# Up products by seven block products in the first and third MLP, behind two ordinary pairs of tiles

## The reference, cut to what matters

```python
# first block                         D_MODEL = SEQ = 1024, D_FF = 4096
hn = rms_norm(h, norm_mlp_w)
h = h + jnp.square(jax.nn.relu(hn @ w_up)) @ w_down
...
# third block
h = rms_norm_3(x, norm2_pre) * (1.0 + scale2) + shift2
f = jnp.square(jax.nn.relu(h @ w_fc1)) @ w_fc2
x = x + gate2 * rms_norm_3(f, norm2_post)
```

## Time and profile before

| | us |
|---|---|
| median of 3 runs | 3459.06 (3456.13 to 3461.45) |
| profiled execution | 3452.28 |
| its span | 3450.5 |
| TensorE busy | 3377.7 (98%) |
| VectorE / ScalarE / GpSimd busy | 1741.4 / 1064.7 / 1238.0 |
| mean granted TensorE clock | 0.991 of full speed |

### The profile page before, as it was taken

The page is one execution under the profiler, slowest core; times in us unless marked ns, Lnnn a source line. Parts: engine busy times, 40 slices in busy tenths (PEclk is TensorE's granted clock), DMA queues, the critical chain, the costliest instruction groups (busy, mean ns, idle before and its releaser), DMA issues.

```text
span 3450.5 us, 39435 instructions
## 1 busy us (share of the span) xinstructions
PE 3377.7 (98%) x16634; PEld 2748.7 (80%) x16634; DVE 1741.4 (50%) x2140; ACT 1064.7 (31%) x1565; POOL 1238.0 (36%) x662
## 2 busy tenths in 40 slices
PE   8999999999999999999999999999999999999998
PEld 6887877887888878765788888888878788888887
DVE  5553375555665468486545445445554631222224
ACT  5432243333112221475332212212332432222222
POOL 3212364555343123313323344344222343333333
PEclk9999999999999999999999999999999999999999
DMA  3112312226454111210212122232211211111113
GB/s 112 37 53 67 119 43 110 106 114 220 177 179 144 69 66 49 74 60 1 86 49 68 58 95 92 68 98 78 86 43 37 77 49 49 49 49 49 48 47 128
DMA packets 94044, 276.51 MB, mean 80 GB/s; under 512 B 13846, under 2 KB 20774, under 8 KB 93740
## 3 DMA queue, kind: packets, MB, share of 16 engines
q1 hardware_dynamic: 93868, 273.99, 23.3%
HBM read 239.18 MB, written 34.78 MB: 79 GB/s over the span
## 4 chain that ended last, share of the span: by engine, by line
PE 91%; DVE 5%; ACT 2%; POOL 1%; DMA 1%; issue 0%; SPq 0%; POOLq 0%; DVEq 0%; ACTq 0%
PE ps L669 25%; PE ps L670 25%; PE ps L672 25%; PE ps L727 3%; PE ps L729 3%; PE ps L728 3%; PE ps L869 1%; PE ps L1128 1%; PE ps L699 1%; PE ps L1177 1%; PE ps L701 1%; PE ps L700 1%; PE ps L1161 1%; DVE P L2711 1%; ACT T L1835 1%; PE ps L1114 0%
## 5 line engine op out<-in xcount | busy, mean ns | idle before, releaser
L3091 POOL TENSOR_TENSOR wlo<-raw,whi 128x1024 fp32r<-128x1024 f32 (+3 forms) x302 | 612.8, 2029 | 1510.2 <-ACT whi L1401 1510.1
L669 PE MATMUL ps<-HH,whi 128*128 128x512 f32 (+1 forms) x2464 | 973.4, 395 | 7.9 <-POOL HL L3097 3.1
L670 PE MATMUL ps<-HL,whi 128*128 128x512 f32 (+1 forms) x2464 | 963.1, 391 | 0.0
L672 PE MATMUL ps<-HH,wlo 128*128 128x512 f32 (+1 forms) x2480 | 767.2, 391 | 0.0
L1401 ACT ACTIVATE whi<-raw 128x1024 fp32r<-128x1024 f32 (+3 forms) x302 | 268.0, 888 | 1249.6 <-PE ps L672 1103.0
L669 PEld LDWEIGHTS ps<-HH,whi 128*128 128x128 f32 (+1 forms) x2464 | 461.7, 187 | 109.6 <-POOL HL L3097 3.5
L672 PEld LDWEIGHTS ps<-HH,wlo 128*128 128x128 f32 (+1 forms) x2480 | 464.3, 187 | 102.3 <-issue 0.6
L670 PEld LDWEIGHTS ps<-HL,whi 128*128 128x128 f32 (+1 forms) x2464 | 461.7, 187 | 98.2 <-issue 1.8
L669 PE MATMUL ps<-GH,whi 128*128 128x512 f32 x1256 | 493.1, 393 | 0.6 <-POOL wlo L3091 0.6
L670 PE MATMUL ps<-GL,whi 128*128 128x512 f32 x1256 | 488.8, 389 | 0.0
L2142 DVE TENSOR_TENSOR X<-ps,X 128x1024 f32<-128x1024 f32 (+1 forms) x155 | 186.2, 1203 | 490.8 <-PE ps L672 489.0
(11 more groups left out here) (440 smaller groups left out, 4166.9 us busy)
## 6 DMA issues: line engine op xcount, KB each, us to landing
raw<-in_w_up SPq DMA_DIRECT2D x76, 512.0 KB, 3.4
raw<-in_w_in SPq DMA_DIRECT2D x70, 512.0 KB, 3.3
raw<-in_w_fc SPq DMA_DIRECT2D x64, 512.0 KB, 3.3
raw<-in_w_down SPq DMA_DIRECT2D x32, 512.0 KB, 4.5
T<-in_w_ada SPq DMA_DIRECT2D x32, 512.0 KB, 4.3
raw<-in_w_fc SPq DMA_DIRECT2D x64, 256.0 KB, 2.7
hsc<-T SPq DMA_DIRECT2D x24, 512.0 KB, 2.6
raw<-in_w_down SPq DMA_DIRECT2D x40, 256.0 KB, 2.6
```

The costliest lines, as they stand in the source:

```text
L669: e.matmul(o_[0:m, half(hf)], whi_[:, k, :], hi[k0 + k][:, half(hf)], start=first, stop=False)
L670: e.matmul(o_[0:m, half(hf)], whi_[:, k, :], lo[k0 + k][:, half(hf)], start=False, stop=False)
L672: i = e.matmul(o_[0:m, half(hf)], wlo_[:, k, :], hi[k0 + k][:, half(hf)], start=False, stop=last)
L3091: e.tensor_tensor(wlo_of(name), raw_of(name), whi_of(name).bitcast(F), SUB).then_inc(*po.inc("lo " + name))
```

## The change

The four operands p4, p5, p6 and p7 get a place of their own in the G buffers, p1, p2 and p3 use the ordinary HH and HL. Both MLPs begin with four ordinary up tiles (two pairs), after which pairs 2 to 15 are block products. The combinations of operands are made between the norm and those pairs. Both then have 40 down tiles in five groups with 8, 8, 8, 4 and 4 input blocks, from hidden tiles that were written to DRAM and read back. The same functions now serve both MLPs, with a relu with bias on ACT in the third. The cut core of the diff:

```diff
+SIZES, FIRST = [8, 8, 8, 4, 4], [0, 8, 16, 24, 28]
+FAST = {f"{t}{f}" for t in DN for f in range(4, 32)}
+SPLIT = ("dn0_0", "fa2_0_0")
...
+    def phases(up, dn, t):
+        for f in range(32):
+            plan(f"{t}{f}", d[up][f])
+        for g in range(5):
+            for m in range(8):
+                plan(f"{DN[t]}{g}_{m}", d[dn][m, :, FIRST[g] * P:(FIRST[g] + SIZES[g]) * P])
...
+        OAT = {"p4": GO, "p7": GO + 16384, "p5": GO + 32768, "p6": GO + 49152}
+        OH = {p: at(f"OH{p}", OAT[p], [P, 4, 512], R) for p in OAT}
+        OL = {p: at(f"OL{p}", OAT[p] + 8192, [P, 4, 512], R) for p in OAT}
+        OF = {p: at(f"OF{p}", OAT[p] + 8192, [P, 4, 512]) for p in OAT}
...
+            for f in range(4):
+                job(f"up{f}", hhs, hls, lambda k: [dv(f"hl2 {k}")], 8, between=norm2 if f == 1 else None)
+                if f == 0:
                     sums("n2", dv("n2 acc7"))
-                elif (p, k) == ("p6", 2):
-                    spread_misc("n2 sp", one, dv("n2 r1"))
-            for n in range(16):
-                fast("up", n, ready=None if n else ready2, between=norm2 if n == 1 else None)
-            for n in range(32):
-                g, j = divmod(n, 8)
-                if (g, j) == (3, 0):
+            fast_all("up")
+            for n in range(40):
+                if n == 32:
                     lend("n3 sq")
-                job(f"dn{g}_{j}", ghs if g % 2 else hhs, gls if g % 2 else hls, lambda k: [either(f"dnl {8 * g + k}")], 8)
+                down("up", n)
                 row_step(n)
...
+            job("fa1_3", hhs, hls, lambda k: [], 8)
+            fast_all("fa1_")
+            for n in range(37):
+                down("fa1_", n)
+            halves(["fa2_4_5", "fa2_4_6", "fa2_4_7"], ghs, gls, lambda k, hf: [either(f"fa2_l {FIRST[4] + k}")], 4, between=tail)
...
+            def operands1(t, g):
+                for i in range(4):
+                    high(f"{t}o5f {i}", OF["p5"][:, i, :], OF["p5"][:, i, :], dv(f"{t}o5d {i}"), scale=g(i))
+                for i in range(4):
+                    q.wait_ge(*ac(f"{t}o5f {i}"))
+                    high(f"{t}o5h {i}", OF["p5"][:, i, :], OH["p5"][:, i, :])
+            def operands2(t, i):
+                for p in ("p6", "p4", "p7"):
+                    high(f"{t}o{p[1]}h {i}", OF[p][:, i, :], OH[p][:, i, :], dv(f"{t}o{p[1]}f {i}"))
...
+            def fast_all(t, bias=None):
+                for w in range(4):
+                    fast_hi(t, w)
+                for n in range(2, 16):
+                    for j in range(7):
+                        if 0 < 7 * (n - 2) + j < 95:
+                            fast_hi(t, 7 * (n - 2) + j + 3)
+                        if n > 2 and j == 0:
...
+                        elif (n, j) == (15, 4):
+                            for k in range(8):
+                                q.wait_ge(*pe(f"{t}15 p4" if k < 4 else f"{t}15 p7"))
+                                high_down(t, k, k, 0)
+                highs(following(t, 0))
+                fast_square(t, 15, 1, bias)
+                fast_square(t, 15, 0, bias)
...
+            def down(t, n):
+                if n < 39:
+                    highs(following(t, n))
+                if next_tile(n):
+                    if n == 0:
+                        q.wait_ge(*pe(f"{DN[t]}0_0"))
+                    high_down(t, *next_tile(n)[:2], 1 - next_tile(n)[2])
...
+            operands1("up", lambda i: col("norm_mlp", i))
+            operands2("up", 0)
+            operands2("up", 1)
+            root("n2", 1024)
+            highs(widx["up2"])
+            operands2("up", 2)
+            operands2("up", 3)
+            to_rt("n2")
+            highs(widx["up3"])
+            fast_all("up")
...
+            for n in range(40):
+                down("up", n)
+                if n > 32:
+                    on_last3(n - 33)
             on_last3(7)
             behind("gg0")
...
+            operands1("fa1_", lambda i: gains[:, 16 + i:17 + i])
+            for i in range(4):
+                operands2("fa1_", i)
             highs(widx["fa1_3"])
             root_half("nx", 1, 512)
...
+            for f in range(4):
+                relu(f)
+            fast_all("fa1_", bias7)
...
+            def operands1(t):
+                for i in range(4):
+                    tt(OF["p5"][:, i, :], X[:, i, half(1)], X[:, i, half(0)], SUB, f"{t}o5d {i}")
+            def operands2(t, i, g):
+                x = X[:, i + 4, :]
+                q.wait_ge(*ac(f"{t}o5f {i}"))
+                stt(OF["p6"][:, i, :], x[:, half(1)], g(i + 4), OF["p5"][:, i, :], MUL, SUB, f"{t}o6f {i}")
+                q.wait_ge(*dv.now())
+                stt(OF["p4"][:, i, :], x[:, half(0)], g(i + 4), OF["p6"][:, i, :], MUL, SUB, f"{t}o4f {i}")
+                stt(OF["p7"][:, i, :], X[:, i, half(0)], g(i), OF["p6"][:, i, :], MUL, SUB, f"{t}o7f {i}")
...
+            def fast_all(t, bias=False):
+                for n in range(2, 16):
+                    if n < 15:
+                        fast_sums(t, n + 1)
+                    fast_step(t, n, "p6", bias)
+                    fast_step(t, n, "p7", bias)
+                    if n == 15:
+                        low_down(t, 1)
+                    fast_step(t, n, "p2", bias)
+                    if n == 15:
+                        low_down(t, 3)
+                    fast_step(t, n, "p4", bias)
+                    fast_step(t, n, "p3", bias)
+                low_down(t, 5)
+                low_down(t, 7)
...
+            q.wait_ge(*pe("wo7"))
+            operands1("up")
+            operands2("up", 0, mlp_gain)
+            operands2("up", 1, mlp_gain)
+            factors("n2")
+            operands2("up", 2, mlp_gain)
+            operands2("up", 3, mlp_gain)
+            q.wait_ge(*ac("n2 rt"))
+            for f in range(4):
+                if f == 3:
+                    fast_sums("up", 2)
+                drain("up", f, False)
+            fast_all("up")
...
+            for k in range(8):
+                q.wait_ge(*at_x6(k))
+            q.wait_ge(*pe("wo37"))
+            operands1("fa1_")
+            for i in range(4):
+                operands2("fa1_", i, fc_gain)
             factors_half("nx", 1)
...
+            def operand_lows(t, i):
+                for p, tok in (("p5", f"{t}o6f {i}"), ("p6", f"{t}o7f {i}"), ("p4", f"{t}o4f {i}"), ("p7", f"{t}o7f {i}")):
+                    q.wait_ge(*dv(tok))
+                    low(f"{t}o{p[1]}l {i}", OF[p][:, i, :], OH[p][:, i, :], OL[p][:, i, :], ac(f"{t}o{p[1]}h {i}"))
...
+            lows(widx["up1"])
+            operand_lows("up", 0)
+            operand_lows("up", 1)
+            lows(widx["up2"])
+            operand_lows("up", 2)
+            operand_lows("up", 3)
+            lows(widx["up3"])
+            fast_all("up")
+            for n in range(40):
+                down("up", n)
...
+            for i in range(4):
+                operand_lows("fa1_", i)
+            lows(widx["fa1_3"])
+            fast_all("fa1_")
+            for n in range(40):
+                down("fa1_", n)
...
+            def fast_all(t):
+                for f in range(4):
+                    behind(f"{t}{f}")
+                    if f:
+                        spill(t, f - 1, v3(T[f - 1][:], 2), dv(f"{t}s{f - 1}"))
+                spill(t, 3, v3(T[0][:], 2), dv(f"{t}s3"))
+                for n in range(2, 16):
+                    loads(widx[f"{t}0"] + 2 * n + 4)
+                    loads(widx[f"{t}0"] + 2 * n + 5)
+                    spill(t, 2 * n + 1, hidden(n)[1], ac(f"{t}sq {2 * n + 1}"))
+                    if n == 14:
+                        for k in range(4):
+                            reload(t, k, k, 0, pe(f"{t}15 p5"))
+                    spill(t, 2 * n, hidden(n)[0], ac(f"{t}sq {2 * n}"))
+                    if n == 14:
+                        for k in range(4, 8):
+                            reload(t, k, k, 0, pe(f"{t}15 p6"))
```

More of the change, by code:

```diff
@@ L676, in step @@
                         i.then_inc(*pe.inc("zu3 late"))
+                    elif n == 3 and name in ("up3", "fa1_3"):
+                        i.then_inc(*pe.inc(name + " half"))
                 return step
@@ L1619, in scalar @@
                 if m:
-                    operands2(m - 1)
-                if m == 7:
-                    fast_hi("up", 0, pe("wo6"))
-                    fast_hi("up", 1, pe("wo6"))
-            fast_hi("up", 2, pe("wo7"))
-            fast_hi("up", 3, pe("wo7"))
-            def copy3(i):
-                high(f"o3f {i}", X[:, i + 4, half(1)], OF["p3"][:, i, :], scale=col("norm_mlp", i + 4))
-            for i in range(3):
-                copy3(i)
-            operands2(7)
-            copy3(3)
@@ L3194, in row_tile @@
                 tt(w_, w_, vec.unsqueeze(2).broadcast_to([P, 8, P]), MUL, name)
-            def mlp(up, dn, sizes, step=None, late=1):
-                n = 0
-                for what, g, j in mlp_plan(up, dn, sizes):
```

(59 more changed lines are left out.)

648 lines of the change are left out of this document (206 added, 442 removed).

## The result

The changed kernel takes **3468.6 us** (median of 10 runs, 3461.9 to 3471.6), the kernel before in the same series 3458.6 (median of 10): ratio **1.0027**, 95% interval 1.0019 to 1.0036. It is 10 us, 0.3%, slower, where 3470 was forecast. Its profiled execution took 3467.9, with a span of 3466.1.

What follows compares the result with a forecast made beforehand. TensorE, busy 98% of the span, was taken to bound the kernel. The terms, +12.2 us for the first MLP and -1.5 for the third, sum to +10.7: median 3470 us (46%), own range 3461 to 3479, wider range 3449 to 3487.

Steps and rivals of the forecast that it cites:

- Matmuls: TensorE's work: two first-MLP pairs become ordinary, +5.4 us; 14 third-MLP pairs lose 12 matmuls each, -38.1 us.
- First MLP, new start: Waits of 1.9, 3.0 and 3.9 us before the spread, up2 and up3, plus slow clock: +13.3 us.
- Third MLP, new start: fa1_3 waits for its low part, queued behind POOL's 16 operand lows: +25.7 us, and +0.5 for the longer wait.
- relu ahead of the first rounding: Third MLP: ACT issues all four relus before the first weight rounding, so TensorE waits 4.7 us plus 1.5 slow: +6.2.
- Up to down: Start of down products, both MLPs: TensorE waits 2.7 us for DVE's low part 5, plus 1.5 slow: +4.2 each.
- gg0: End of first MLP: gg0's weights are prepared late, so TensorE idles 9.4 us, plus 2 slow: +11.4.
- No cost taken: Settled third-MLP pairs, spills, reloads and the third's down additions to X were charged nothing.
- rival D: 4%: third MLP's block products don't run as 84 matmuls, relu or sums late, 0.5 us x 14 beyond C: 3491.
- A: Faster, 16%: operands made nearly free of contention, POOL's 16 lows taking below 21 us: 3447 us.
- B: No change, 20%: contention as forecast, but DVE's low parts reach down products in time and first start costs 9: 3457.
- C: Far slower, 14%: each pair of DVE and POOL operations costs 1.98 us, lengthening both starts; DVE late in down tiles: 3484.
- The ends of the range: Sums of all terms' bounds: low ends stated as -13 us (3446), high ends as +33 (3492).

Runs made afterwards that it cites:

- the serial run: Changed kernel, with POOL beginning the third MLP's operand low halves only after DVE's last of twelve combinations: 3467.9 us, ratio 1.0028 to the kernel before.

## Why the prediction was right

**Matmuls** (+5.4, -38.1): the count fell by the 144 forecast and the pace stayed. Right.

**First MLP, new start** (+13.3, for old waits of 22.1): the place and releaser of each wait were right, the sizes 1.9, 3.0 and 3.9 against 0.97, 2.08 and 4.51, of which only one lies in the 2 to 4 that was to show it right. Their sum is 7.6, not 8.8, and the stage gained 6.3 rather than 3.4. By the stage the new start cost 22.1 - 6.3 - 5.4 = 10.4, not 13.3 (8.4 by the two traces in which the stage is shortest). 1.2 of the difference are the waits' sum; the rest is the 1.5 us that I charged behind each of them: the matmul behind the wait of 2.08 lasts 0.50 and only that behind the one of 4.51 lasts 0.77. The waits of 0.97 and 2.08 cost little beyond themselves.

**Third MLP, new start** (+25.7 + 0.5): 25.9. fa1_3 was forecast 31.4 us behind the reciprocal (2794.2 - 2762.8), measured 31.6, in the two waits named, spread and then wlo. The term was sized right, its account not fully: I wrote that POOL decides, and in the changed kernel it does end the wait, but fa1_0's bank, which the prediction never names, comes free only when DVE's first drain ends, 24.8 behind the reciprocal. POOL was later still, at 31.5, so the forecast held without it; what an order alone could win it would have missed.

**relu ahead of the first rounding** (+6.2): the wait is 4.97 (4.7 forecast), and taking it away gave 6.5. Right.

**Up to down** (+4.2 each): the waits are 2.84 and 3.57 for low part 5, 2.7 forecast. The stages grew by 2.1 and 6.1, together 8.2 against 8.4, but the split between the MLPs was wrong. 2.5 of the third's 6.1 lie beyond the wait, and 1.7 of these are the slow clock behind it that the windows view shows; the other 0.8 wasn't tried. In the first MLP the clock stays at full speed behind the 2.84, so the 1.5 charged there was not due.

**gg0** (+11.4): a wait of 9.52 against 9.4; undone alone it gave 9.7 up to gg0's first matmul, with slow clock behind that, and 12.8 by medians. Right.

**No cost taken** in settled pairs, for spills or reloads: 259 of 259 us busy. Right, so rival D is out.

**Rivals.** A wanted POOL's 16 lows in under 21 us: fifteen took 23.09, and the serial run shows DVE's part doubled by them. B wanted a first start of 9, which 10.4 comes near, and DVE's low parts in time, which they were not. C wanted each pair of operations at 1.98 us. Both at once took 26.7 us where one after the other took 31.1, and the third start 31.6 where C gives 34: contention as in the earlier trace rows, and not more. The Trainium skill (SBUF — State Buffer, section "SBUF: two separate sides") has the loser blocked for the whole instruction. Twelve combinations and sixteen lows would by that gain nothing from running at once. The runs show a gain, but a small one: of the 4.4 us some 2 are DVE's squares, three of which fell beside lows in the serial run and one in the changed kernel, each stretching its low from 1.27 to about 2.25. So some 2.4 us are gained in 26.7, and C's mechanism was nearer than its price.

**The ends of the range.** With the bounds as the prediction states them, the low ends sum to -10.4 and the high ends to +29.9, not to -13 (which has rival A's smaller terms) and +33. The forecast itself adds up.

## What to carry to other kernels

New work on helper engines before a product is paid for at the seam, not in the steady state: add up both engines' queues there at their contended durations, and put what the next product of TensorE needs (weights, factor, the bank it writes) ahead of what only the one after it needs. Clear a queue's wait and read the next releaser's name: here POOL's low part hid a bank, the bank hid the low half and the sums of the next weights, and behind those stood the plain amount of work. A loop that prepares "the next tile" ends one tile early, as here before gg0; check who prepares the one behind the loop. Such seams made this change a loss of 10 us, and their order alone makes it a gain: 24 us below the kernel before by medians, 0.6% by the ratio.

## What the runs showed of the hardware

While POOL subtracts, DVE slows by what it reads. In the serial experiment an operation on 128x1024 that reads SBUF alone (T<-T) takes 2.29 us, and one whose first input is in PSUM (T<-ps,RT) 1.21, both beside POOL. With POOL idle T<-T takes 1.23, in the run without low halves:

```profile
2791.00 1.23 DVE L2109 TENSOR_TENSOR T<-T 128x1024 f32<-128x1024 f32 x1 [1.22 <-ACT T L2074]
```

So the drains cost nothing extra beside POOL, the squares 1.1 us each, and a low half beside a square about 1.0. The Trainium skill (SBUF — State Buffer, section "SBUF: two separate sides") gives the lock to DVE operations with two SBUF inputs, and this agrees in kind.

I had not expected two stages that nobody touched to move by as much as the change is worth. In three of the variants the wait before one small matmul early on was 6.2 us instead of 1.1, and their first stage was 484.3 to 486.5 instead of 476.6 to 482.3. A single profiled time can't judge a 10 us change in this kernel; stage times between landmarks can.
